# Three score steps ahead of the small sum in the sample attention of a hybrid decoder step

## The reference

```python
q_abs = einsum('bthn,chn->bthc', q_nope, w_uk)
s_past = einsum('bthc,bsc->bhts', q_abs, c_past) + einsum('bthr,bsr->bhts', q_rope, kr_past)
s_new = einsum('bthc,buc->bhtu', q_abs, c_new) + einsum('bthr,bur->bhtu', q_rope, kr_new)
p = softmax(concatenate([s_past, s_new], -1) * scale)
o_lat = einsum('bhts,bsc->bthc', p[..., :past], c_past) + einsum('bhtu,buc->bthc', p[..., past:], c_new)
```

## Time and profile before

| | |
|---|---|
| median of 3 runs | 1068.41 us (1066.91 to 1068.78) |
| span of the profiled execution | 1064.8 us |
| between the median and that span | 3.6 us |
| PE busy in the span | 990.8 us |
| DVE busy | 668.9 us |
| ACT busy | 387.6 us |
| the sample attention | from about 411 to 551 us |

### The profile page before, as it was taken

How to read it: one execution, slowest core, us unless ns; L and a number is a source line. 1 busy time by engine, 2 the same in 40 slices (tenths; PEclk the granted TensorE clock), 3 DMA queues, 4 the chain that set the end, 5 groups by cost and what they waited for, 6 DMA issues and landing times.

```text
span 1064.8 us, 22625 instructions
## 1 busy us (share of the span) xinstructions
PE 990.8 (93%) x9310; PEld 913.0 (86%) x9310; DVE 668.9 (63%) x1052; ACT 387.6 (36%) x854; POOL 69.0 (6%) x76
## 2 busy tenths in 40 slices
PE   4999999999999996777789999999999999999995
PEld 3899999978888884454469999999999999999995
DVE  7558654765564556666565748798764244767567
ACT  3323433323233242121332313356562113656321
POOL 0000000000000033444400000000000000000000
PEclk9999999999999998789999999999999999999998
DMA  8522356040405167777816664142333342241633
GB/s 247 163 68 76 102 143 158 5 120 22 120 21 146 40 198 258 235 261 259 261 53 231 210 171 111 49 118 82 88 89 89 89 119 79 80 114 53 181 110 131
DMA packets 179381, 137.09 MB, mean 129 GB/s; under 512 B 19219, under 2 KB 163448, under 8 KB 179032
## 3 DMA queue, kind: packets, MB, share of 16 engines
q1 hardware_dynamic: 166442, 93.56, 31.4%
q0 software_dynamic: 10368, 37.75, 10.7%
q10 hardware_dynamic: 2502, 4.78, 1.2%
HBM read 124.27 MB, written 11.90 MB: 128 GB/s over the span
## 4 chain that ended last, share of the span: by engine, by line
PE 78%; DVE 12%; issue 4%; another core or an unknown queue 2%; ACT 2%; DMA 1%; ACTq 0%; DVEq 0%
PE PS L1958 34%; PE PS L2185 9%; PE PS L2632 8%; PE PS L2694 6%; PE PS L1969 3%; PE PS L2528 3%; PE PS L2356 3%; PE PS L2411 2%; DVE pages_T L1431 2%; DVE w_lo L1173 2%; PE PS L2223 2%; PE PS L2212 1%; PE PS L2200 1%; PE PS L2284 1%
## 5 line engine op out<-in xcount | busy, mean ns | idle before, releaser
L1958 PE MATMUL PS<-x_hi,w_hi 128*128 128x268 f32 x744 | 164.5, 293 | 2.7 <-DVE x_lo L1220 1.4
L1173 DVE TENSOR_TENSOR w_lo<-w_raw,w_hi 128x2048 fp32r<-128x2048 f32 (+3 forms) x65 | 125.9, 1936 | 60.6 <-ACT w_hi L660 48.8
L1958 PE MATMUL PS<-x_hi,w_lo 128*128 128x268 f32 x744 | 160.2, 287 | 0.0
L1958 PE MATMUL PS<-x_lo,w_hi 128*128 128x268 f32 x744 | 160.2, 287 | 0.0
L660 ACT ACTIVATE w_hi<-w_raw 128x2048 fp32r<-128x2048 f32 (+3 forms) x59 | 94.5, 1601 | 149.5 <-PE PS L1958 90.2
L1958 PEld LDWEIGHTS PS<-x_hi,w_hi 128*128 128x128 f32 x744 | 120.3, 189 | 6.0 <-issue 2.4
L1958 PEld LDWEIGHTS PS<-x_lo,w_hi 128*128 128x128 f32 x744 | 119.7, 189 | 0.0
L1958 PEld LDWEIGHTS PS<-x_hi,w_lo 128*128 128x128 f32 x744 | 119.4, 189 | 0.0
L2185 PE MATMUL PS<-x_hi,w_hi 128*128 128x268 f32 x256 | 78.5, 307 | 0.0
L611 POOL DMA_INDIRECT pages_c<-in_cache_kv_latent_dram,page_rows x48 | 46.4, 966 | 426.9 <-DVE w_uk_T L1478 372.6
L2356 PE MATMUL PS<-pages_T,q_blocks 128*32 128x128 f32 x1024 | 49.0, 297 | 26.2 <-issue 15.9
(11 more groups left out here) (373 smaller groups left out, 2311.7 us busy)
## 6 DMA issues: line engine op xcount, KB each, us to landing
w_raw<-in_w_ffn_in_dram SPq DMA_DIRECT2D x44, 512.0 KB, 4.5
w_raw<-in_w_in_dram SPq DMA_DIRECT2D x37, 512.0 KB, 7.0
w_raw<-in_w_ffn_out_dram SPq DMA_DIRECT2D x28, 320.0 KB, 3.7
w_raw<-in_w_o_dram SPq DMA_DIRECT2D x12, 512.0 KB, 6.3
w_raw<-in_w_ffn_out_dram SPq DMA_DIRECT2D x16, 384.0 KB, 4.1
gate_scratch<-gate_out ACTq DMA_DIRECT2D x8, 536.0 KB
gates<-gate_scratch SPq DMA_DIRECT2D x8, 536.0 KB, 8.9
x_T_scratch<-x_sum_T SPq DMA_DIRECT2D x1, 2144.0 KB, 7.6
```

Of the source, the lines that this page charges most:

```text
L1173: V.tensor_tensor(WL[:, par, 0:nk], RAW[:, par, 0:nk], WH[:, par, 0:nk].bitcast(F32), ALU.subtract).then_inc(s_wsplit, 1)
L1958: last = T.matmul(PS[:, bank, 0:HALF], w[:, par, k, m * P:(m + 1) * P], x[:, k0 + k, half * HALF:(half + 1) * HALF], start=start and k == ...
```

## The change

In `sample(b)`, for an entry that has one in front of it, the steps 0 to 2 of the second half of the scores are issued right before the small sum of the entry in front. The other six steps stay where all nine were, behind `turn_parts(0)` and the chunks weighed there. No other engine's program is changed.

```diff
                 if b >= 2:
                     latent_turn(b - 2)
                 if prev:
+                    score_half(b, 1, range(3))
                     sum_spread(1 - par)
                     weigh_chunk(b - 1, 0)
                     weigh_chunk(b - 1, 1)
@@
                 if prev:
                     for c in range(2, NCH if last else 3):
                         weigh_chunk(b - 1, c)
-                score_half(b, 1)
+                score_half(b, 1, range(3 if prev else 0, 9))
                 if prev and not last:
                     weigh_chunk(b - 1, 3)
                 turn_parts(1)
```

## The result

The changed kernel takes 1089.72 us (median of 4 runs, 1088.09 to 1093.35), the kernel before beside it 1068.6 us: a ratio of 1.0185, 95% interval 1.0156 to 1.0214. It is 21 us slower by the medians, 19.8 by the ratio. The forecast was 1083.3 us, 14.9 over a kernel before of 1068.41; the ratio times that is 1088.2 us, at the upper end of the forecast range.

A forecast was written before the change was run, and what follows sets the result against it. TensorE's wait for VectorE's last transposes (T7) was taken to bound the sample attention loop. Span 1064.8 + 14.2 moved work + 0.7 tile shapes = 1079.7 us, 1083.3 with what lies around the span; range 1076 to 1089.

The forecast's parts named there:

- The bound: Sample attention, 18 to 19 us per entry: a loop of waits, with TensorE waiting for VectorE's last transposes before the second half.
- T7: Moment VectorE's last transposes of an entry's chunks 6 and 7 end, letting the second half start; forecast not to move.
- The moved work is paid behind the wait: Entries 1 to 7: small sum, chunks 0 to 2 and turn_parts(0) fall behind the transposes, costing 14.2 us in all.
- rival C: TensorE's longer stands lower its clock in entries 2 to 6: 3.8 to 7.5 us more, 1087 to 1091; chance 0.14.
- A: Sample attention: the work moved behind the wait is paid in full, 1083.3 us; chance 0.62.
- rival B: Moved work fills the second half's stalls from GpSimd; half the cost of entries 2 to 6 goes, 1077 us; chance 0.18.
- The ends: Costs forecast outside the repeating entries 3 to 6: entry 1 0.7 us, entry 2 3.2 us, entry 7 1.7 us of waiting.
- Tile shapes: Small sum between 128*32 groups: two more tile shape changes, 0.1 us per entry, 0.7 in all, bounds 0 to 2.
- What hides the later reciprocal: VectorE's later reciprocal and four transposes end at T7 + 6 to 7.5 us, hidden before the new scores at T7 + 9.2.
- D: Faster: the steps fill TensorE's stand before the small sum, gaining at most 5.1 us, 1063.3; chance 0.03.
- E: No difference: GpSimd's loads set the pace of the stage and the loop has slack against them; chance 0.03.
- Around the span: 3.6 us between the profiled span of 1064.8 us and the median of 1068.41 us, carried unchanged.

The follow-up runs named there:

- e6: Changed kernel with VectorE's latent_out put behind the turning of chunks 6 and 7: 1077.99 against 1072.24 us for the kernel before, ratio 1.0062.
- e10: Changed kernel with only the wait for turned chunks 4 to 7 ahead of the small sum, all nine steps back together: 1045.94 us, ratio 1.0156 to the kernel before.
- e9: The changed kernel, unedited, timed again in a later set: 1049.25 against 1031.88 us for the kernel before, ratio 1.0187.
- e11: Changed kernel with three idle matmuls of 512 columns in the stand of entries 2 to 7: 1043.24 us, ratio 1.0103 to the kernel before.
- e2: Changed kernel with the steps moved in entries 1 and 7 alone: 1036.31 us, ratio 1.0022 to the kernel before.

## Why the prediction was right, and where it was off

**The bound.** Right. The chain over T7 (`latent_turn`, `latent_out`, two transposes, second half) sets the turn. T7 stayed where it was against `latent_turn`, 5.2 us, and e6, which loosens just this link, is 15 us less slow than the 21 of the result (with the reserve said there).

**The moved work is paid behind the wait.** Right, and shown by e10 beside e9: the wait moved without any step costs 14.1 of 17.4 us by the medians, and in the traces of the two the stage is equally long. The steps themselves are innocent. They carry the wait, and the wait is what matters.

**The size.** Off by 5 to 6 us: 14.9 forecast, 21.1 measured by the medians and 19.8 by the ratio. The term at fault is the clock. The sum took every duration from rows mostly at 2.4 GHz, and gave the clock to rival C alone, with 0.14. In the trace after, TensorE resumed at 1.2 GHz behind the stand of each of entries 2 to 7, and the work there took 4.4 to 5.0 us instead of 3.0. e11 against e9 prices it at 6.0 us by the medians of one set, 4.6 by the traces of the stage; both ran on the faster ground, and on the ground of the result no run prices it. Rival C's mechanism was right and was no alternative to A: it came on top. The measured time is where C put it, 1087 to 1091; it is inside the forecast range only because that was drawn up into C's part. A row that hinted at it was on hand: the clock was 0.91 in a turn whose longest stand was 1.6 us, and the forecast stand was three times as long. It was no more than a hint, as the next turn had the same stand at 1.00.

**Part of it came back.** Moved work (2.15) and clock (1.4 to 2) would add 4.1, 4.1, 3.9 and 3.5 us to entries 3 to 6; the tables show 3.54, 2.56, 3.42 and 3.62. In entry 6, whose second half comes after GpSimd's last issue, nothing came back. In entry 4 some 0.75 of the 1.5 us is what the low clock had already cost the kernel before there. For the rest, see the second half of entry 4. It without its first 24 records takes from 508.52 to ACT's release at 511.80, and with them (1.5) 4.8 us, although these are at the low clock, against 5.6 before. Two of GpSimd's issues fall on it now, three did before. That is rival B in part, half a microsecond to one in entries 3 to 5; it is read off the traces, no run separates it.

**The ends.** Entry 1: 0.7 forecast. From the end of its last transpose to the next `latent_turn` are 13.8 us before (440.83 to 454.63) and 16.3 after (439.19 to 455.52), 2.5 more; what the other 1.8 us are stays open. Entry 2: 3.2 forecast, 2.15 measured; the clock was low there before already. Entry 7: 1.7 forecast, 4.46 measured in the turn, again the clock:
```profile
561.40 1.51 PE L2356 MATMUL PS<-pages_T,q_blocks 128*32 128x128 f32 x24 [2.55 <-DVE pages_T L1431]
562.84 0.60 PE L2392 MATMUL PS<-sm,square_consts 128*128 128x8 f32 x2
...
565.52 2.69 PE L2411 MATMUL PS<-pages_c,p_sample 128*32 128x256 f32 x32
```
The wait grew as forecast, but the work behind it runs at the low clock, and 32 weighing records take 2.69 us there. At the full clock 47 took 2.81 in the kernel before.

**Tile shapes.** 0.7 us were allowed; nothing shows, 0.03 us in entry 5 and 0.06 over the stage in e10 against e9.

**What hides the later reciprocal.** Right: VectorE waited for the scores as before (L1527), also with its four transposes released 2.1 us behind the end of the last one.

**D and E** fell: no entry's transposes were ahead of the sum, and the loop had no slack.

**Around the span.** The forecast carried 3.6 us between span and time. In every run that lists both it is 2.1 to 2.3 (1088.09 us for the span of 1085.9); the rest was the spread between executions. It doesn't enter the difference that was forecast.

## What to carry to other kernels

A step that carries a wait is dear by its wait, not by its work: before moving it ahead, find out when that wait is satisfied, and count everything behind it in the queue as waiting too. Small work in front of a long wait (here the sum and three chunks) may be what fills a wait that can't be shortened. And when an edit turns two short stands into one long one, price the work behind it at the low clock from the start: in this kernel the clock was low behind all six stands of the changed kernel (4.6 us, the last 2.55), and on the faster ground behind five of six of 2.54 us.

## What the runs showed of the hardware

TensorE can be held up while GpSimd issues indirect loads (0.94 us each), at points where the profile shows nothing that it waits for: with plain loads of the same bytes the kernel before is 40.7 us faster, and the second half of the scores takes 2.3 instead of 5.6 us. That didn't hold everywhere. In three of the four sets of experiments the unchanged kernel takes 1032 to 1034 us, as long as the one with plain loads in the fourth. With indirect loads in one of those sets, and the second half as in the kernel before (e2, entry 4):
```profile
471.99 1.74 PE L2356 MATMUL PS<-pages_T,q_blocks 128*32 128x128 f32 x56
...
473.54 0.94 POOL L611 DMA_INDIRECT pages_c<-in_cache_kv_latent_dram,page_rows  x1 [0.30 <-issue]
473.93 0.43 PE L2356 MATMUL PS<-pages_T,q_blocks 128*32 128x128 f32 x8 [0.19 <-issue]
474.14 0.43 PE L2356 MATMUL PS<-rope_T,q_blocks 128*32 128x128 f32 x8
```
The issues are as long and as many, and TensorE hardly stops: 2.6 us. So neither the issues nor the scattered pages are enough by themselves to hold TensorE up. What differs between the two grounds, and by what path a load reaches TensorE, no run here settles.

The granted clock fell within a single stand and stayed low for what came next. In entry 4 after, it was 1.00 in the first 2.7 us of the stand and 0.50 over the 4.95 us of matmuls behind it. A filler of three idle matmuls (2.82 us) kept it at 1.00 over six turns (e11).
